# A hybrid encoder block on one core: merge and output stage in one block, and a new order of the routing and of the first expert

## What is computed

```python
merged = jax.nn.sigmoid(g_attn) * (attn @ w_attn_branch) + jax.nn.sigmoid(g_lru) * (lru @ w_lru_branch)
mix = merged @ w_out
x = x + gate1[:, None, :] * mix
h2 = modulate(rms_norm(x, norm2_w[l]), shift2, scale2)
# router: softmax over 16 experts, each expert takes its 128 best tokens
affinity = jax.nn.softmax(h2 @ w_router, axis=-1)
gates, idx = lax.top_k(jnp.swapaxes(affinity, 1, 2), 128)
# for each expert: xe = h2[idx]
he = jax.nn.silu(xe @ w_gate) * (xe @ w_up)
ys = (he @ w_down) * gates[..., None]      # added to the rows idx
x = x + gate2[:, None, :] * ffn
```

## Time and profile before

| | us |
|---|---|
| median of the runs (2144.91 to 2146.18) | 2145.29 |
| the profiled execution | 2147.01 |
| its span | 2145.2 |
| TensorE busy / ScalarE / DVE / POOL | 2061.2 / 1244.0 / 1625.4 / 175.7 |
| granted TensorE clock, mean | 0.986 |

### The profile page before, as it was taken

The page is one execution under the profiler, slowest core; times in us unless marked ns, Lnnn a source line. Parts: engine busy times, 40 slices in busy tenths (PEclk is TensorE's granted clock), DMA queues, the critical chain, the costliest instruction groups (busy, mean ns, idle before and its releaser), DMA issues.

```text
span 2145.2 us, 26158 instructions
## 1 busy us (share of the span) xinstructions
PE 2061.2 (96%) x10061; PEld 1695.9 (79%) x10061; DVE 1625.4 (76%) x1608; ACT 1244.0 (58%) x1162; POOL 175.7 (8%) x128
## 2 busy tenths in 40 slices
PE   5999989999999999897889999999999999999998
PEld 4777977888888888785668888888888888888886
DVE  5777656588865532555899898989898999888986
ACT  4422155377764322334557777777777777777774
POOL 3000000000000000000531011011110111001100
PEclk9999989999999999998999999999999999999999
DMA  8665120301112211236689999999999999999994
GB/s 281 174 193 164 40 59 2 83 27 44 45 58 90 79 49 59 81 118 226 246 313 389 389 384 386 394 389 389 375 384 392 388 386 379 389 384 388 384 377 163
DMA packets 245966, 511.66 MB, mean 239 GB/s; under 512 B 8028, under 2 KB 64776, under 8 KB 245896
## 3 DMA queue, kind: packets, MB, share of 16 engines
q1 hardware_dynamic: 236688, 484.91, 61.5%
q0 software_dynamic: 6608, 19.40, 3.5%
q10 hardware_dynamic: 2600, 6.38, 1.3%
HBM read 487.07 MB, written 16.78 MB: 235 GB/s over the span
## 4 chain that ended last, share of the span: by engine, by line
PE 50%; DVE 1%; POOL 0%; ACT 0%; issue 0%; DVEq 0%; POOLq 0%
PE ps_gu L2455 32%; PE ps_down L2455 16%; PE ps_turn L2450 2%; POOL h_lo L2416 0%; DVE h_lo L2268 0%; DVE third_split L2268 0%; DVE acc L2317 0%; ACT third_split L2234 0%; DVE const L2314 0%; DVE const L2313 0%; DVE acc L2312 0%; POOL out_x L2435 0%; DVE moe_h_lo L2278 0%; DVE moe_x_lo L2278 0%; ACT moe_gate L2244 0%
## 5 line engine op out<-in xcount | busy, mean ns | idle before, releaser
L2268 DVE TENSOR_TENSOR h_lo<-tiles,h_hi 128x2048 fp32r<-128x2048 f32 x250 | 561.5, 2288 | 68.0 <-ACT h_hi L2234 61.4
L2234 ACT ACTIVATE h_hi<-tiles 128x2048 fp32r<-128x2048 f32 x252 | 468.7, 1911 | 80.0 <-PE ps_down L2455 42.9
L2268 DVE TENSOR_TENSOR third_split<-tiles,third_split 128x2048 fp32r<-128x2048 f32 x124 | 278.6, 2288 | 37.0 <-ACT third_split L2234 35.8
L2234 ACT ACTIVATE third_split<-tiles 128x2048 fp32r<-128x2048 f32 x128 | 238.1, 1911 | 50.3 <-PE ps_down L2455 24.9
L2455 PE MATMUL ps_gu<-h_hi,moe_x_hi 128*128 128x512 f32 x640 | 252.0, 394 | 7.9 <-DVE moe_x_lo L2278 5.4
L2455 PE MATMUL ps_gu<-h_hi,moe_x_lo 128*128 128x512 f32 x640 | 250.2, 391 | 0.0
L2455 PE MATMUL ps_gu<-h_lo,moe_x_hi 128*128 128x512 f32 x640 | 250.0, 391 | 0.0
L2455 PE MATMUL ps_gu<-third_split,moe_x_hi 128*128 128x512 f32 x768 | 239.8, 393 | 1.7 <-POOL third_split L2416 1.6
L307 PE MATMUL ps_projected<-h_hi,hi_ring 128*128 128x512 f32 x480 | 187.6, 391 | 1.1 <-PEq L891 0.5
L307 PE MATMUL ps_projected<-h_hi,lo_ring 128*128 128x512 f32 x480 | 186.8, 389 | 0.0
L307 PE MATMUL ps_projected<-h_lo,hi_ring 128*128 128x512 f32 x480 | 186.8, 389 | 0.0
(11 more groups left out here) (388 smaller groups left out, 3834.9 us busy)
## 6 DMA issues: line engine op xcount, KB each, us to landing
tiles<-in_w_gate SPq DMA_DIRECT2D x64, 2048.0 KB, 11.3
tiles<-in_w_up SPq DMA_DIRECT2D x64, 2048.0 KB, 11.7
tiles<-in_w_down SPq DMA_DIRECT2D x64, 2048.0 KB, 11.6
tiles<-in_w_ada SPq DMA_DIRECT2D x24, 1024.0 KB, 8.4
tiles<-in_w_in SPq DMA_DIRECT2D x17, 1024.0 KB, 5.2
tiles<-in_w_in SPq DMA_DIRECT2D x16, 512.0 KB, 5.4
tiles<-in_w_lru_branch SPq DMA_DIRECT2D x8, 1024.0 KB, 5.0
v<-v ACTq DMA_DIRECT2D x48, 128.0 KB, 2.5
```

Of the source, the lines that this page charges most:

```text
L2234: nc.scalar.activation(half(w_hi(t), i), half(raw_tile(g, t), i), ACT.Copy).then_inc(hi_ready, 1)
L2268: nc.vector.tensor_tensor(half(w_lo(t), i), half(raw_tile(g, t), i), half(w_hi(t), i).bitcast(F32), ALU.subtract).then_inc(lo_ready, 1)
```

## The change

The two blocks become one: `stage_merge` turns into `merge_parts`, whose five queues `stage_out` runs ahead of its own. `ps_mix`, `ps_tr`, `ps_log` and `ps_choice` are now the PSUM banks of the merge. All three rows are spread right behind the last gate's products, row 2 first. The last gate's tanh, gating and add are cut into columns 0 to 127 and the rest; m of tile 0 goes between them, and so does the second half of w_out's low part. The x loads are issued behind the weight fetches. x1 and rows change places in `lru_t`.

The rank is computed in another form: only later tokens are compared, one DVE instruction a tile with its sum, straight from PSUM; TensorE adds the token's number and the counts (with a matrix of minus ones), which gives 1023 minus the rank, and the slot table counts down. Its tables are loaded late: `later` by SP in the last tile ahead of the weight tiles, `token` by POOL after the last x1; both go into the buffers of x. Idle transposes are put between. POOL makes the low part of expert 0's tile 0 in this stage, and gathers x of expert 0 here into `attn_t`. Picked values go into the buffer of x1, so DVE waits for its stores.

In expert 0 POOL takes tiles 0, 2, 3, 4, 7 and 10; DVE's order is written anew; three list copies go to ScalarE; the list transposes come after tile 9 instead of 8; the high part of x comes ahead of the copy of the gate 2 row, and SP's fetches wait for the first gather.

The diff, cut to its core (the moved but unchanged lines of the merge are left out):

```diff
--- before.py
+++ after.py
...
-    c[:, C_UPPER:C_SLOT] = p[None] > p[:, None]
-    c[:, C_SLOT] = p
+    c[:, C_LATER:C_TOKEN] = np.arange(T)[None] > p[:, None]
+    c[:, C_SLOT] = T - 1 - p
...
+FIRST_COLS, LATER_COLS = slice(0, P), slice(P, T)
...
+    i = parts[0]
+    low = b.nc.vector.tensor_tensor(g.h_lo[:, 2 * n + i, :], b.unit("out", n)[:, i, :],
+                                    g.h_hi[:, 2 * n + i, :].bitcast(F32), ALU.subtract)
+    if i:
+        low.then_inc(b.out_read, 1)
...
+        def tanh(p):
+            act.wait_ge(b.pair_done, item(p) + 1)
+            if p >= 4:
+                act.wait_ge(merged_done, 2 * (p // 4) - 1 + p % 2)
+            for cols in (FIRST_COLS, LATER_COLS) if p == n_gates - 1 else (slice(0, T),):
+                nc.scalar.activation(gate(p)[:, cols], gate_out(p)[:, cols], ACT.Tanh, scale=0.5).then_inc(gate_tanh, 1)
...
+        def gated(c, cols=slice(0, T), part=0):
+            p = 4 * (c // 2) + 2 + c % 2
+            dve.wait_ge(gate_tanh, p + 1 + part)
+            nc.vector.scalar_tensor_tensor(out=gate(p)[:, cols], in0=gate(p)[:, cols], scalar=1.0, in1=g.merged[:, c, cols],
+                                           op0=ALU.add, op1=ALU.mult).then_inc(lru_gated, 1)
...
+        def add(c, cols=slice(0, T), part=0):
+            p = 4 * (c // 2) + c % 2
+            dve.wait_ge(lru_gated, c + 1 + part)
+            dve.wait_ge(attn_read, c + 1)
+            nc.vector.tensor_tensor(g.merged[:, c, cols], gate(p)[:, cols], gate(p + 2)[:, cols], ALU.add
+                                    ).then_inc(merged_done, 1)
...
+        for n in range(2):
+            out_low(b, dve, g, n)
+        out_low(b, dve, g, 2, (0,))
+        gated(7, FIRST_COLS)
+        add(7, FIRST_COLS)
+        gated(7, LATER_COLS, 1)
+        g.add_last = lambda: add(7, LATER_COLS, 1)
...
-        rows = lambda r: spare[:, r, :] if r < 2 else g.attn_t[:, 0, :]
+        rows = lambda r: spare[:, 2 + r, :] if r < 2 else g.attn_t[:, 0, :]
         h2_t = g.attn_t[:, 1, :].rearrange("p (c n) -> p c n", n=P)
-        x, x1, h2 = spare[:, 2:4, :], spare[:, 4:6, :], spare[:, 6:8, :]
+        x, x1, h2 = spare[:, 4:6, :], spare[:, 0:2, :], spare[:, 6:8, :]
...
-        row_banks = lambda r: (ps_log[:, :], ps_choice[:, :]) if r == 1 else (ps_tr[:, 0, :], ps_tr[:, 1, :])
+        row_banks = lambda r: ((ps_tr[:, 0, :], ps_tr[:, 1, :]), (ps_log, ps_choice), (ps_mix[:, 0, :], ps_mix[:, 1, :]))[r]
+        ROW_ORDER = [2, 0, 1]
+        rows_done = lambda r: 2 * ROW_ORDER.index(r) + 2
         @block.sync
         def _(sp):
-            sp.dma_start(order[:, :], d["const"][:, C_END:C_ALL]).then_inc(g.rest_in, 16)
+            merge.sync(sp)
+            sp.wait_ge(merge.branch_ps, KC)
...
+                    sp.dma_start(later, d["const"][:, C_LATER:C_TOKEN]).then_inc(g.rest_in, 16)
...
+            merge.scalar(act)
+            act.wait_ge(merge.merged_done, KC)
             m_high(0)
+            row(2)
             out_high(b, act, g, 3)
-            nc.scalar.activation(ones[:, :], const[:, C_ONE:C_ONE + 1].to_broadcast([P, P]), ACT.Copy).then_inc(sem["column_read"], 1)
+            nc.scalar.activation(minus[:, :], const[:, C_ONE:C_ONE + 1].to_broadcast([P, P]), ACT.Copy, scale=-1.0)
             row(0)
             row(1)
+            act.wait_ge(merge.merged_done, KC + 1)
             m_high(1)
-            row(2)
...
             tile_high(0, 0)
-            act.wait_ge(g.choice_ps, 1)
-            for h in range(2):
-                nc.scalar.activation(column[:, col_half(h)], ps_column[:, h, :], ACT.Copy).then_inc(sem["column_read"], 1)
             tile_high(0, 1)
             act.wait_ge(sem["aff_ps"], 1)
             act.wait_ge(sem["logit_ps"], TT)
             for n in range(1, EARLY_SPLIT):
                 for i in range(2):
                     tile_high(n, i)
+            act.wait_ge(sem["compared"], TT)
+            act.wait_ge(sem["stored_x1_0"], 8 * TT)
+            nc.scalar.activation(column_copy, column, ACT.Copy).then_inc(sem["column_read"], 1)
         @block.gpsimd
         def _(pool):
+            merge.gpsimd(pool)
             nc.gpsimd.memset(router[:, :, E:ROWS], 0.0).then_inc(sem["padded"], 1)
+            pool.wait_ge(sem["x1_ready"], 2 * TT)
+            pool.dma_start(token, d["const"][:, C_TOKEN:C_ALL]).then_inc(sem["token_in"], 16)
+            for i in range(2):
+                pool.wait_ge(g.hi_ready, i + 1)
+                nc.gpsimd.tensor_tensor(half(tile_lo[:, 0, :], i), half(raw_tile(g, 0), i), half(tile_hi[:, 0, :], i).bitcast(F32),
+                                        ALU.subtract).then_inc(g.lo_pool, 1)
+            for t in range(2):
+                pool.wait_ge(sem[f"stored_h2_{t}"], 8 * TT)
+            pool.wait_ge(g.chosen, FIRST_TOKENS)
+            nc.gpsimd.indirect_dma_start(g.attn_t[:, 0, :], None, h2_dram,
+                                         bass.IndirectOffsetOnAxis(g.slot_token[:, 0:1], 0)).then_inc(g.gathered, 16)
         @block.vector
         def _(dve):
+            merge.vector(dve)
             chain = g.dve_chain = Chain(dve, g.dve_chain.sem, g.dve_chain.n)
             def m_low(t):
                                         m_hi[:, t % 2, :, :].bitcast(F32), ALU.subtract).then_inc(sem["m_lo"], 1)
             m_low(0)
+            out_low(b, dve, g, 2, (1,))
             out_low(b, dve, g, 3)
+            g.add_last()
             m_low(1)
-            dve.wait_ge(sem["rows_ready"], 2)
+            dve.wait_ge(sem["rows_ready"], rows_done(0))
...
             dve.wait_ge(g.rest_in, 32)
-            dve.wait_ge(sem["column_read"], 3)
+            dve.wait_ge(g.choice_ps, 1)
             for t in range(TT):
-                start, end = t * P, (t + 1) * P
                 if t >= 4:
                     dve.wait_ge(g.choice_ps, t - 2)
-                nc.vector.tensor_scalar(below(t)[:, 0:end], column[:, 0:end], first_value(t), None, ALU.is_lt
-                                        ).then_inc(sem["compared"], 1)
-                if t < TT - 1:
-                    nc.vector.tensor_scalar(below(t)[:, end:T], column[:, end:T], first_value(t), None, ALU.is_le
-                                            ).then_inc(sem["compared"], 1)
-                nc.vector.scalar_tensor_tensor(out=same[:, start:end], in0=column[:, start:end], scalar=first_value(t),
-                                               in1=upper, op0=ALU.is_equal, op1=ALU.mult).then_inc(sem["compared"], 1)
-            dve.wait_ge(g.choice_ps, TT + 2)
-            ranks = ps_rank.rearrange("p a n -> p (a n)")
+                nc.vector.scalar_tensor_tensor(out=beats(t), in0=column[:, t * P:], scalar=first_value(t), in1=later[:, 0:T - t * P],
+                                               op0=ALU.is_le, op1=ALU.mult, accum_out=beaten[:, t:t + 1]
+                                               ).then_inc(sem["compared"], 1)
+            dve.wait_ge(g.choice_ps, TT + 1)
+            dve.wait_ge(sem["stored_x1_1"], 8 * TT)
             chain(nc.vector.scalar_tensor_tensor(out=picked_out, in0=ranks, scalar=slot, in1=token, op0=ALU.is_equal,
                                                  op1=ALU.mult, accum_out=token_f[:, :]))
-            chain(nc.vector.tensor_copy(g.slot_token[:, 0:1], token_f[:, :]))
-            chain(nc.vector.scalar_tensor_tensor(out=picked_out, in0=ranks, scalar=slot, in1=column, op0=ALU.is_equal,
+            nc.vector.tensor_copy(g.slot_token[:, 0:1], token_f[:, :]).then_inc(g.chosen, 1)
+            dve.wait_ge(sem["column_read"], 1)
+            chain(nc.vector.scalar_tensor_tensor(out=picked_out, in0=ranks, scalar=slot, in1=column_copy, op0=ALU.is_equal,
                                                  op1=ALU.mult, accum_out=g.slot_gate[:, 0:1]))
...
+            merge.tensor(pe)
+            pe.wait_ge(g.gate_tanh, merge.n_gates - 1)
+            row(2)
+            pe.wait_ge(merge.attn_read, KC)
             row(0)
             row(1)
+            pe.wait_ge(sem["rows_ready"], rows_done(2))
...
-                    pe.wait_ge(sem["rows_ready"], 2)
-                    row(2)
                     pe.wait_ge(sem["rows_ready"], 6)
+                    pe.wait_ge(g.gate_tanh, merge.n_gates + 1)
                 else:
                     route(t - 1)
+            def hold_clock(count):
+                for n in range(count):
+                    nc.tensor.transpose(ps_choice[:, (1 + n % 3) * P:(2 + n % 3) * P], ident, ident)
             sum_groups(TT - 2)
+            hold_clock(18)
             turn_h2(TT - 1)
+            hold_clock(4)
             route(TT - 1)
             sum_groups(TT - 1)
+            pe.wait_ge(sem["token_in"], 16)
+            pe.wait_ge(sem["x1_ready"], 2 * TT)
+            for h in range(2):
+                nc.tensor.matmul(ps_rank[:, h, :], ident[:, 0:1].to_broadcast([P, P]), token[:, col_half(h)], start=True, stop=False)
+            hold_clock(4)
             pe.wait_ge(sem["shifted"], 2)
```

(83 more changed lines are left out.)

523 lines of the change are left out of this document (252 added, 271 removed).

## The result

| | before | after |
|---|---|---|
| median of the runs taken side by side (4 each) | 2145.53 us | 2130.92 us |
| profiled execution, and its span | 2147.01, 2145.2 us | 2131.41, 2129.6 us |

The ratio is 0.9932, 95% interval 0.9917 to 0.9947: 14.6 us faster, where 24.7 were forecast, and 1.9 us above the forecast's range. The two kernels measured again beside the experiments gave 0.9931 and 0.9935.

A forecast was written before the change was run, and what follows sets the result against it. TensorE, busy 96% of the span, was taken to bound the kernel, so only its idle stretches before expert 1 counted. A and B 8.2, C 6.1 and D 10.4 sum to 24.7 us: 2120.6 us from 2145.3, range 2115.5 to 2129.

The forecast's parts named there:

- A: Between merge and output stage: without the block boundary, mix starts at 883.3 instead of 888.38, gaining 5.1 us.
- B: After the first mix tile: row 2 is already spread ahead, so TensorE's pause there goes, gaining 3.1 us.
- Pick: Routing to expert 0: the pick waits for the x1 store and starts at 1013.6, 0.3 us earlier than before.
- Rival 1: Token table lands late, at 9.6 us with a slow clock: pick 3.8 us later, 2124.4 us; chance 20%.
- C: Routing to expert 0's first product: new rank form and earlier turn of x, first product at 1023.7, gaining 6.1 us.
- D: Expert 0: new order and held clock remove stalls, 75.2 us from its start to expert 1's first product, gaining 10.4 us.
- hand run of the tiles: Expert 0: the new order of POOL and DVE tiles run through with old durations, TensorE ending tile 10 at 1089.2.
- the hold that the prediction took from the Trainium skill: Choosing expert 1's tokens: DVE's multiplication of two SBUF tiles waits for POOL's tile 10, to 1086.9 instead of 1086.3.
- Rival 2: Expert 0 keeps its stalls, by a misplaced POOL tile or an 8.7 us gather: 2131.0 us, half 2125.8; chance 12%.

The follow-up runs named there:

- e7: Changed kernel with row 2 spread behind mix tile 0 again, rows 0 and 1 left behind the last gate; 2133.86 us, ratio 0.9944.
- e3: Changed kernel with both tables of the token choice loaded early, behind the first loads of x; 2127.79 us, ratio 0.9916.
- e2: Changed kernel with POOL's gather for expert 0 replaced by a plain SP load of 512 KB, leaving out the choice of its rows; ratio 0.9917.
- e10: e9 plus expert 0's gather moved to the next block's start, with DVE's first split held until it is issued; 2124.97 us, ratio 0.9902.
- e12: Changed kernel with DVE held until expert 1's gather is issued, and SP issuing weight tile 14 behind that gather; 2126.96 us, ratio 0.9918.
- e6: Changed kernel with 44 idle transposes on TensorE ahead of its wait for expert 1's rows; 2130.48 us, ratio 0.9925.
- e11: e10 plus DVE held behind expert 1's gather, weight tile 14 held until it landed, clock-holding transposes, gate 2's row copied ahead of x; 2119.30 us, ratio 0.9873.
- e4: Changed kernel with DVE meant to wait for expert 1's gather issue through a bare semaphore count, but not actually held; ratio 0.9931.
- e1: Changed kernel with the gather of expert 0's rows moved to be POOL's first instruction in the next block; 2130.13 us, ratio 0.9933.
- e9: e3 plus picks written into x instead of x1, without the waits for the x1 stores; 2127.72 us, ratio 0.9916.
- e8: Changed kernel with DVE held behind expert 1's gather by a count that a small POOL memset makes; 2131.40 us, ratio 0.9930.
- e14: e11 without any hold of weight tile 14; 2123.70 us, ratio 0.9896.
- e13: e11 with weight tile 14 issued right behind expert 1's gather instead of held until it landed; 2117.73 us, ratio 0.9872.

## Why the prediction was wrong

- **A and B** (8.2 forecast, 8.9 measured). Right, and for the reasons given: the rows at 5.3 us instead of 5.8, since the 1.95 us of one row overlap with what follows; back to back they stand 1.78 us apart (876.70 to 878.48). B's own size is smaller than its row suggests (e7); the sum of both is what counts.
- **Pick** (0.3 forecast, 0.2 measured). Right: it waits for the x1 store, and the store is late by the bytes of the tables (e3 gives back 2.7). Rival 1 was met half way: TensorE did wait 2.4 us for the token table, but the pick waits longer.
- **The failed step of C** was "The gather, issued inside the old stage at 1015, lands at 1019.3 by the 4.2 us row: off the path". I let the next block begin beside it. The block cannot begin before POOL's gather has landed, and that costs 3.9 us (e2) of the 5.2 that were missing. Another 0.8 is the turn of x, 1.75 us (half clock) instead of the 1.0 taken; the other 0.5 lie in the gate rows (3.75 us instead of 3.5) and around the block's start. In e10, where TensorE had stood still for 3.8 us ahead of the block instead of 8.5, it took 1.09; in e7, with 8.5 us, 1.05 all the same, so the idle time alone does not decide it.
- **The failed term of D** is the gather's landing. The 5.9 us of the earlier trace rows was taken as a property of a gather in expert 0. SP's weight tiles stand beside it in the timelines of SP and POOL, first of the kernel before:

```profile
1094.24 0.37 SPq L2146 DMA_DIRECT2D tiles<-in_w_up  x1
...
1097.70 2.30 POOL L2400 DMA_INDIRECT moe_x<-h_rows,slot_token  x1 [3.49 <-DVE slot_token L2335]
```

and then of the kernel after:

```profile
1082.41 0.37 SPq L2192 DMA_DIRECT2D tiles<-in_w_gate  x1
...
1083.38 2.89 POOL L2447 DMA_INDIRECT moe_x<-h_rows,slot_token  x1 [1.00 <-DVE slot_token L2386]
```

The tile before had gone out 3.5 us ahead of the gather; it landed 8.1 us after its issue, and the rows 1.3 us behind it. The tile after goes out 1.0 us ahead and lands in 7.9; with the same 1.3 behind it the rows need 8.2, as measured. Undone by the order of issue in e12, this gave 2.9 us. The new order frees the tile and the tokens at the same moment, and I did not ask what SP would issue then.

So the 5.3 us that D lacks (80.5 against 75.2) are 2.3 of landing, 2.1 of turn and tile 11 (8.2 us instead of the 6.1 forecast) and 0.9 of a gather issued 64.15 us after the first product instead of 63.2, of which 0.8 lie between the tokens and the issue and were left out. Of the 2.1 some 1.7 are clock (e6 gives 1.6 back), and 0.35 a slip of the sum: its own durations, 1.0 for the turn and 5.45 for the tile, make 6.45. The hand run of the tiles stood. That expert 0 took 75.5 in e11, near the forecast 75.2, is partly luck: there the gather is issued 1.0 us late as well, lands in 4.2 us instead of the 5.9 assumed, and turn and tile 11 take 7.1 us.
- DVE's product of two SBUF tiles (1080.34 in the chain above) took 2.07 us where its neighbours take 0.17, and ended with POOL's tile: the hold that the prediction took from the Trainium skill. The same page, "SBUF — State Buffer" (the trap on DMAs issued by GpSimd), also says that GpSimd cannot write descriptors while DVE holds the port; it names a two-port mode there, and further down counts a `tensor_tensor`, DVE's operation here, as one that did not stall a DMA in its probe. The measurement decides: this case shows a delay of that kind for a DVE operation with two SBUF inputs that was already running when the issue began (0.11 us ahead of it in e4): an issue of 2.89, 3.04 and 2.54 us beside one, ending about 0.9 us behind the end of DVE's first half, against 0.98 to 1.05 without. That the port is the reason was not measured. The earlier trace rows hint at it: DVE's two halves start at 1096.84, and the gather issued at 1097.70 took 2.30 us (shown above).
- Rival 2, half of D lost, came true in time (2125.8 by itself), but not by a POOL tile out of its place; its other half, a gather of 8.7 us, was near the 8.2 measured. With C's loss of 5.2 on top that is 2131.0, and 2130.9 was measured.

Not settled: what makes the half clock last 3.7 us behind the turn's start in one trace and 5.7 in another, and why the rows' first packets wait some 3 us while a tile moves. Nor was the landing of POOL's gather at the block's end tried with the block boundary removed altogether.

## What to carry over

A transfer that a change moves ahead of a block's end is waited for there if it is a gather of POOL's; moving it across is worth little until what slows its issue on the other side is moved too (e1 against e10). A landing time is not a property of a transfer: note beside it what was issued ahead of it and by how much, and let the small transfer on the critical path go first. Behind a new wait of TensorE price the next work at both clocks.

## What the runs showed of the hardware that I had not expected

- The block's end waits for POOL's gather to land (it begins 0.5 to 0.6 us behind the landing in eleven traces: the three of the kernel after, e3 to e9 and e12), and not for a load that SP has under way (e2: begin 1.6 us ahead of its landing).
- A semaphore count that follows a gather in POOL's program, made by no operation, came before the gather ran (e4); attached to a memset it came behind it (e8).
- 512 KB of gathered rows need 7.5 to 8.6 us where another queue issued a 2 MB tile 1.0 us ahead of them, about as long as the tile does (they land 0.6 us ahead of it in e14 and 1.0 to 1.4 behind it where the issue is slow), and 4.7 where the tile is issued 1.2 us behind them (4.5 in e13). Their first packet moves 3.0 to 3.4 us behind the end of the issue where the tile was 1.0 us ahead (seven traces, 3.1 in the kernel after, 3.3 in e8), 1.2 in the kernel before, whose tile was 3.5 us ahead, and 0.7 on idle engines and in e12 and e13. The token table, a plain load of POOL's issued among SP's weight tiles, waited 3.4 (issue ended at 984.32, first packet at 987.7).
- The Trainium skill says in "DMA: Bandwidth & Descriptors" (queues, rings and completion order) that each DMA engine takes turns between its queues; with equal shares the order should matter little, by my estimate at most the 1.35 us of the rows' own bytes. The trace agrees only from the rows' first packet on: in e8 at 1088 to 1091 they and the tile have 44 and 60% of the engines. The same section says that a completion count lands only after every earlier write of that engine, across its queues. That is not where the 2.9 us lie, since in e8 no packet of the rows had moved by 1088. What holds the first packet is open.
